# A two-layer hybrid decoder on one core: reciprocal roots of all norms taken by square root and reciprocal instead of by logarithm and exponential

## The chip, the core and the metric

The kernel runs on one core of a Trainium2 chip. The core has a matrix engine (TensorE, PE in the profile), a vector engine (VectorE, DVE), an engine for activation functions (ScalarE, ACT), a general engine (GpSimd, POOL) and queues that start DMA transfers (SyncE, SP). Each engine runs its own instructions in order and waits on semaphores for the others. The metric is the time of one execution on the device in microseconds; less is better.

## The reference, cut to what matters

The model has 512 tokens of width 1024 and two layers. Each layer normalizes its input, multiplies it by one wide matrix, runs four token mixers on groups of the result's columns, merges them under gates, multiplies by another matrix, normalizes and adds to the input; then comes a feed-forward part with two more norms.

```
h = rms_norm(x, norm_mix_pre[l]);  proj = h @ w_in[l]
y_a = hgrn2_mixer(...)      # ends in a norm over each head of 64
y_b = dsa_mixer(...)        # top-k attention, no norm
y_c = rwkv7_mixer(...)      # normalizes its keys, ends in a norm over each head
y_d = fox_mixer(...)        # attention with a forget gate, no norm
x = x + rms_norm(merged @ w_out[l], norm_mix_post[l])
hm = rms_norm(x, norm_mlp_pre[l]);  u = relu(hm @ w_up[l])
x = x + rms_norm(square(u) @ w_down[l], norm_mlp_post[l])

def rms_norm(t, g, eps=NORM_EPS):
    y = t * lax.rsqrt(jnp.mean(t * t, axis=-1, keepdims=True) + eps)
    return y * g
```

## The kernel before, in words

Everything is held transposed: features on the 128 partitions, tokens along the free dimension, so x is eight tiles of 128x512. Each matrix product in float32 is split into three products of rounded parts (high times high, low times high, high times low): lines 611, 612 and 613, on operands named `_hi` and `_lo`. Weights arrive in chunks of 128x1024; ScalarE writes their high part (line 1180), GpSimd their low part in four pieces (line 1641).

The large products ("dense" steps) are dealt out among the small ones of the mixers by a written table: `schedule()` and `FILL` say how many dense steps TensorE does between two small steps of a mixer. So TensorE mostly has dense work while VectorE and ScalarE prepare what a mixer's next small product needs, and stands idle only where the dense steps given to a place run out before that preparation is done.

A reciprocal root is needed at eight places in each layer:

- **Entry** (`norm_rstd(1, 1, 5, ...)` on ScalarE): 128x512 numbers for the norm of the layer's input. TensorE transposes the result (line 778), VectorE scales the first projections with it (lines 1804 and 1802, `taken_raw`), which also frees the PSUM banks that hold them.
- **Mixer A's norm** (lines 1394, 1395): 128x1024. VectorE writes the variances at line 1909 and multiplies with the result at line 1912, then finishes mixer A's output and turns to the rotations of mixer B (lines 1924 to 1926, TensorE's part at line 857).
- **Mixer C's keys** (lines 1444, 1445): 128x1024. VectorE goes on at line 2085 and builds the operands that TensorE transposes at line 915.
- **Mixer C's norm** (lines 1492, 1493): 128x1024, VectorE goes on at line 2157 and ends with `y_ready`, which TensorE needs before the products of branch 2.
- **After the mixers** (`norm_rstd(2, ...)` and `norm_rstd(3, ...)`): 128x256 each, one for each half of the tokens. VectorE's `residual_enter` scales (line 1744), adds to x (line 1749) and writes the low part of the next operand (line 1753), ScalarE its high part (line 1165).
- **After the feed-forward part** (`norm_rstd(4, ...)` and `norm_rstd(5, ...)`): the same, 128x256 each. In the first layer they lead into the next layer's entry, in the second into the output.

At each place ScalarE takes the logarithm (line 1271, for the first and the last two kinds), waits for its own result, and takes the exponential of minus one half of it (line 1272). ScalarE holds one set of function tables at a time; the compiler puts an `ACT_TABLE_LOAD` ahead of a function that the loaded set lacks. In the program as compiled such a load stands between the logarithm and the exponential at all eight places.

Of the kernel before, what the change touches and what calls it, by code (L numbers as in the profile page):

```python
# [12 lines left out]
LAYERS, T, D = 2, 512, 1024  # L13
# [254 lines left out]
def trunk_kernel(nc, x_in, wproj, wmerge, wrest, par_in, con_in, mask_in, rope_in, out):  # L268
    f32, f32r, u8 = mybir.dt.float32, mybir.dt.float32r, mybir.dt.uint8
    ALU, ACT = mybir.AluOpType, mybir.ActivationFunctionType  # L270
# [3 lines left out]
    with ctx:  # L274
        def sb(name, shape, dt=f32):
            return ctx.enter_context(nc.sbuf_tensor(name, shape, dt))
# [26 lines left out]
        slab = sb("slab", [P, 20, FT * T])  # L303
# [17 lines left out]
        rstd = sb("rstd", [P, T])  # L321
# [8 lines left out]
        ps = [ctx.enter_context(nc.psum_tensor(f"bank{i}", [P, 512], f32)) for i in range(8)]  # L330
# [70 lines left out]
        dve_took = signal("dve_took_dense", DVE0 + 16 * QUARTERS)  # L401
        relu_done = signal("relu_ready", 8 * QUARTERS)
        hid_hi = signal("hidden_hi_ready", 8 * QUARTERS)
        dve_step = signal("dve_step", 205)
        act_step = signal("act_step", 9)

        in_sq = signal("entry_squared", 2 * KT)
        entry_added = signal("entry_squares_added", 1)
# [8 lines left out]
        v_ready = signal("eps_term_ready", 1)  # L417
        o_total = signal("out_squares_added", 3)
        d_total = signal("down_squares_added", 2)
        rstd_done = signal("rstd_by_exp", 5)  # L420
        rstd_tr = signal("rstd_transposed", 1)
        rstd_col = signal("rstd_column_ready", 1)

# [26 lines left out]
        a_r = signal("a_rstd_ready", 1)  # L450
# [42 lines left out]
        c_kkr = signal("c_key_rnorm_ready", 1)  # L493
# [25 lines left out]
        c_rr = signal("c_rstd_ready", 1)  # L519
# [630 lines left out]
        def _(act):  # L1150
            fn = act.activation

            def link(ins, sig=act_step):

                ins.then_inc(*sig.up())
                act.wait_ge(*sig.at(L, sig.count))

            act.dma_start(par[:, 0:NPAR], par_in[0:1, :, 0:NPAR].rearrange("a p n -> (a p) n")).then_inc(par_first, 16)
            act.dma_start(con[:, 0:NHEAD], con_in[:, 0:NHEAD]).then_inc(ones_loaded, 16)
            act.preload_act_table(ACT.Ln)  # L1160
            act.wait_ge(par_first, 16)

            def split_x(m, n, hi, gain):
# [12 lines left out]
            with act.Fori(0, LAYERS) as L:  # L1176
# [49 lines left out]
                def take(place_):  # L1226
                    take_steps(TAKEN_TO[place_], REACH[place_] - TAKE_LAG)
# [40 lines left out]
                def norm_rstd(total, done, b, cols=slice(0, T), **bias):  # L1268

                    act.wait_ge(*sumsq.at(L, total))  # L1270
                    link(fn(rstd[:, cols], ps[b][:, cols], ACT.Ln, scale=1.0 / D, **bias))
                    fn(rstd[:, cols], rstd[:, cols], ACT.Exp, scale=-0.5).then_inc(*rstd_done.up())
                    assert rstd_done.count == done

                def attention(which, pt):
                    base = 16 * which
# [59 lines left out]
                act.dma_start(npre[:, :], par_in[bass.ds(act.snap(L * -1 + (LAYERS - 1)), 1), :, PC["pre"]:PC["pre"] + KT]  # L1336
                              .rearrange("a p n -> (a p) n")).then_inc(par_loaded.handle, 16)
                par_loaded.count += 32
                act.preload_act_table(ACT.Ln)
                split_to(INDEX[("aq", 0)] + 1)  # L1340
                norm_rstd(1, 1, 5, bias=C("eps", n=1))

# [46 lines left out]
                for t in range(FT):  # L1389
                    fn(S(19, t), S(18, t), ACT.Square).then_inc(*a_sq.up())  # L1390
                take(("a_norm", 0))
                act.preload_act_table(ACT.Ln)
                act.wait_ge(*a_var.at(L, 1))
                link(fn(slab[:, 0, :], slab[:, 0, :], ACT.Ln))
                fn(slab[:, 0, :], slab[:, 0, :], ACT.Exp, scale=-0.5).then_inc(*a_r.up())


                take("B")
# [3 lines left out]
                   scale=1.0 / 16.0).then_inc(*b_iwc.up())  # L1402
# [41 lines left out]
                link(fn(slab[:, 5, :], slab[:, 5, :], ACT.Ln))  # L1444
                fn(slab[:, 5, :], slab[:, 5, :], ACT.Exp, scale=-0.5).then_inc(*c_kkr.up())
# [44 lines left out]
                act.preload_act_table(ACT.Ln)  # L1490
                act.wait_ge(*c_vv.at(L, 1))
                link(fn(slab[:, 5, :], slab[:, 5, :], ACT.Ln))
                fn(slab[:, 5, :], slab[:, 5, :], ACT.Exp, scale=-0.5).then_inc(*c_rr.up())


                take("D")
# [40 lines left out]
                hi_part(o0 + 5)  # L1537
                out_taken(3)
                hi_part(o0 + 6)
                act.preload_act_table(ACT.Ln)  # L1540
                for m in range(4, KT):
                    out_taken(m, 0)
                    if m < 7:
# [54 lines left out]
                for j in range(13):  # L1598
# [5 lines left out]
                act.preload_act_table(ACT.Ln)  # L1604
                square(4, 0)
                hi_part(entry_order(CHUNKS + 0))
                square(5, 0)
# [81 lines left out]
        def _(dve):  # L1689
            tt, ts, stt = dve.tensor_tensor, dve.tensor_scalar, dve.scalar_tensor_tensor  # L1690

            def link(ins, sig=dve_step):

                ins.then_inc(*sig.up())
                dve.wait_ge(*sig.at(L, sig.count))
# [25 lines left out]
            with dve.Fori(0, LAYERS) as L:  # L1721
# [10 lines left out]
                def norm_lo(m):  # L1732

                    dve.wait_ge(*h_norm_hi.at(L, m + 1))
                    tt(hn[1][:, m, :], tmp[:, m % 4, :], hn[0][:, m, :].bitcast(f32), SUB).then_inc(*h_norm.up())

                def residual_enter(done, src, gain, part, split_gain, first, n, between={}):

                    cols = HALF[n]
                    dve.wait_ge(*rstd_done.at(L, done))  # L1740
                    base = [0] * KT

                    def scale(m):
                        stt(src[:, m, cols], src[:, m, cols], pcol(gain, m), rstd[:, cols], MUL, MUL).then_inc(*dve_step.up())  # L1744
                        base[m] = dve_step.count

                    def add(m):
                        dve.wait_ge(*dve_step.at(L, base[m]))
                        tt(x[:, m, cols], x[:, m, cols], src[:, m, cols], ADD).then_inc(*x_tiles.up())  # L1749

                    def lo(m):
                        dve.wait_ge(*h_hi.at(L, first + m + 1))
                        stt(part[1][:, m, cols], x[:, m, cols], gain_col(split_gain, m), part[0][:, m, cols].bitcast(f32), MUL, SUB)\  # L1753
                            .then_inc(*h_ready.up())
                    for m in range(KT + 2):
                        if m in between:
                            between[m]()
                        if m < KT:
                            scale(m)
                        if 0 < m <= KT:  # L1760
                            add(m - 1)
                        if m > 1:
                            lo(m - 2)
# [56 lines left out]
                tt(col[:, 6, 0:2], lb0, col[:, 5, 0:2], SUB)  # L1820
                tt(col[:, 6, 2:4], lb1, col[:, 5, 0:2], SUB).then_inc(*lb_in.up())
                ts(col[:, 5, 6:8], par[:, PC["ka"]:PC["ka"] + FT], -1.0, 1.0, MUL, ADD)
                dve.wait_ge(*rstd_done.at(L, 1))
                for i in range(2):
                    taken_raw("af", i)
                dve.wait_ge(*lb_exp.at(L, 1))
# [82 lines left out]
                    ins = ts(S(0, t), ps[4 + t][:, :], 1.0 / HD, EPS, MUL, ADD)  # L1909
                ins.then_inc(*a_var.up())  # L1910
                dve.wait_ge(*a_r.at(L, 1))
                link(tt(slab[:, 18, :], slab[:, 18, :], slab[:, 0, :], MUL))
                link(stt(slab[:, 18, :], slab[:, 18, :], pcol("hgw"), slab[:, 3, :], MUL, MUL))
                split(S(18), y[0][:, 0, :, :], y[1][:, 0, :, :], y_ready)
# [167 lines left out]
                dve.wait_ge(*c_exd.at(L, 1))  # L2082
                tt(slab[:, 6, :], slab[:, 6, :], slab[:, 12, :], MUL)
                dve.wait_ge(*c_kkr.at(L, 1))
                link(tt(slab[:, 4, :], slab[:, 4, :], slab[:, 5, :], MUL))
                link(tt(slab[:, 3, :], slab[:, 3, :], slab[:, 4, :], MUL))
                stt(slab[:, 7, :], slab[:, 7, :], -1.0, slab[:, 4, :], MUL, MUL)
# [261 lines left out]
```

## Time and profile before

| | |
|---|---|
| time, median of 3 runs | 2081.71 us (2080.02 to 2085.82) |
| the profiled execution's own time | 2085.43 us |
| its span, first to last instruction | 2083.5 us |
| TensorE's mean granted clock | 0.984 of full speed |
| TensorE busy | 1988.8 us (95% of the span) |
| VectorE, ScalarE, GpSimd busy | 997.4, 832.9, 999.1 us |

The busy shares are means over stages with different limits: an engine that is busy half of the time may still be the one that the others wait for in a given stretch. The idle time that the profile puts down to an instruction says which engine's result ended the wait. "L1272" is line 1272 of the kernel before.

### The profile page before, as it was taken

What the parts mean: (1) busy time and instruction counts of PE and PEld (TensorE: products, weight loads), DVE (VectorE), ACT (ScalarE), POOL (GpSimd) and SP (SyncE); (2) the same over time, 40 slices, a digit from 0 to 9 for tenths busy, and PEclk for the clock granted to TensorE, in tenths of its full rate; (3) what the DMA queues carried; (4) which work ended last, traced back from release to release, by engine and by line L of the source; (5) the groups of instructions that cost most, each with busy time, mean ns of one, the idle gap of its engine ahead of it and who ended that gap; (6) DMA issues with size and microseconds to landing.
All of it is one profiled execution on the core that took longest, in us unless ns stands there. A gap on an engine that the chain in (4) does not pass through costs nothing.

```text
span 2083.5 us, 34716 instructions
## 1 busy us (share of the span) xinstructions
PE 1988.8 (95%) x12444; PEld 1593.4 (76%) x12444; DVE 997.4 (48%) x1844; ACT 832.9 (40%) x1407; POOL 999.1 (48%) x1225
## 2 busy tenths in 40 slices
PE   7899999999999999999998999999999989999996
PEld 7786856777787888888887767577776788888885
DVE  6737976333433713223486479753234454223135
ACT  6434356324534422222463344642355263222235
POOL 4335525223566555557624444251253755555574
PEclk9999999999999999999999999999999999999998
DMA  5122311112132133233312223111121222333323
GB/s 177 60 82 69 94 52 41 42 32 62 62 108 73 60 105 101 91 101 93 111 48 72 82 71 92 42 46 37 32 71 62 91 82 72 111 96 96 101 91 122
DMA packets 53736, 163.09 MB, mean 78 GB/s; under 512 B 5312, under 2 KB 17728, under 8 KB 53312
## 3 DMA queue, kind: packets, MB, share of 16 engines
q1 hardware_dynamic: 52416, 158.09, 23.7%
q10 hardware_dynamic: 1152, 2.86, 0.4%
q8 instruction: 93, 1.52, 0.3%
q14 instruction: 75, 0.61, 0.1%
HBM read 158.83 MB, written 2.10 MB: 77 GB/s over the span
## 4 chain that ended last, share of the span: by engine, by line
issue 53%; POOL 44%; DVE 1%; POOLq 1%; ACT 1%; DMA 0%; PE 0%; SPq 0%; DVEq 0%; ACTq 0%
POOL w_lo L1641 38%; POOL slab L1665 3%; POOL slab L1686 1%; POOL wx_lo L1641 1%; POOL rstd L1654 1%; POOLq L1671 0%; POOL slab L1668 0%; DMA wx_raw<-wproj 0%; DVE slab L1744 0%; POOLq L1646 0%; DVE u_lo L1753 0%; ACT u_hi L1171 0%; ACT u_hi L1165 0%; POOL w_lo L1635 0%; DVE x L1749 0%
## 5 line engine op out<-in xcount | busy, mean ns | idle before, releaser
L1641 POOL TENSOR_TENSOR w_lo<-w_raw,w_hi 128x256 fp32r<-128x256 f32 x1104 | 853.5, 805 | 1046.9 <-ACT w_hi L1180 765.2
L611 PE MATMUL bank<-hn_hi,w_hi 128*128 128x512 f32 (+1 forms) x1312 | 538.7, 411 | 0.0
L613 PE MATMUL bank<-hn_hi,w_lo 128*128 128x512 f32 (+1 forms) x1312 | 508.5, 388 | 0.0
L612 PE MATMUL bank<-hn_lo,w_hi 128*128 128x512 f32 (+1 forms) x1312 | 508.5, 388 | 0.0
L611 PE MATMUL bank<-u_hi,w_hi 128*128 128x512 f32 (+1 forms) x864 | 306.5, 355 | 11.1 <-DVE u_lo L1767 5.7
L613 PE MATMUL bank<-u_hi,w_lo 128*128 128x512 f32 (+1 forms) x864 | 303.4, 351 | 0.0
L612 PE MATMUL bank<-u_lo,w_hi 128*128 128x512 f32 (+1 forms) x864 | 303.2, 351 | 0.0
L611 PEld LDWEIGHTS bank<-hn_hi,w_hi 128*128 128x128 f32 x1312 | 248.4, 189 | 71.0 <-issue 24.8
L613 PEld LDWEIGHTS bank<-hn_hi,w_lo 128*128 128x128 f32 x1312 | 248.4, 189 | 51.0
L1571 ACT ACTIVATE w_hi<-w_raw 128x1024 fp32r<-128x1024 f32 x120 | 127.3, 1061 | 399.3 <-DMA w_raw<-wrest 399.3
L612 PEld LDWEIGHTS bank<-hn_lo,w_hi 128*128 128x128 f32 x1312 | 249.1, 190 | 42.5 <-issue 3.4
L611 PEld LDWEIGHTS bank<-u_hi,w_hi 128*128 128x128 f32 x864 | 164.0, 190 | 37.7 <-DVE u_lo L1767 7.6
L612 PEld LDWEIGHTS bank<-u_lo,w_hi 128*128 128x128 f32 x864 | 164.1, 190 | 21.8 <-issue 0.5
L613 PEld LDWEIGHTS bank<-u_hi,w_lo 128*128 128x128 f32 x864 | 163.9, 190 | 21.4
L1180 ACT ACTIVATE w_hi<-w_raw 128x1024 fp32r<-128x1024 f32 x156 | 164.2, 1055 | 33.4 <-DMA w_raw<-wrest 17.1
L2230 DVE TENSOR_TENSOR slab<-slab,bank 128x512 f32<-128x512 f32 x56 | 38.5, 688 | 245.3 <-PE bank L613 245.3
L2221 DVE TENSOR_TENSOR tmp<-bank,tmp 128x512 f32<-128x512 f32 x64 | 44.2, 691 | 188.8 <-ACT tmp L1577 188.8
L1469 ACT ACTIVATE slab<-bank 64x128 f32<-64x128 f32 x160 | 43.7, 273 | 130.0 <-PE bank L962 128.1
L962 PEld LDWEIGHTS bank<-slab 64*64 64x64 f32 x1920 | 63.4, 134 | 32.1 <-issue 32.1
L1240 ACT ACTIVATE tmp<-bank 128x512 f32<-128x512 f32 x64 | 37.4, 600 | 119.1 <-PE bank L613 109.0
L2128 DVE COPY_PREDICATED slab<-msk,bank 128x256 f32<-128x256 uint8 x48 | 23.6, 491 | 115.6 <-PE bank L962 92.4
L962 PE MATMUL bank<-slab 64*64 64x32 f32 x1920 | 71.1, 220 | 2.1 <-DVE slab L2117 1.0
(346 smaller groups left out, 2853.5 us busy)
## 6 DMA issues: line engine op xcount, KB each, us to landing
w_raw<-wrest SPq DMA_DIRECT2D x140, 512.0 KB, 3.5
w_raw<-wmerge SPq DMA_DIRECT2D x80, 512.0 KB, 3.5
w_raw<-wproj SPq DMA_DIRECT2D x60, 512.0 KB, 3.5
wx_raw<-wproj SPq DMA_DIRECT2D x6, 512.0 KB, 5.3
slab<-rope ACTq DMA_DIRECT2D x2, 1024.0 KB, 5.4
wx_raw<-wrest SPq DMA_DIRECT2D x4, 512.0 KB, 5.0
out<-x SPq DMA_DIRECT2D x4, 512.0 KB, 3.0
x<-x_in SPq DMA_DIRECT2D x2, 512.0 KB, 9.8
```

Source lines behind the costliest of these rows:

```text
L611: mm(o_, stat[0], mov[0], start=first, stop=False)
L612: mm(o_, stat[0], mov[1], start=False, stop=False)
L613: return mm(o_, stat[1], mov[0], start=False, stop=last)
L962: ins = mm(packed(o_, n), stat[rs, cs_], halves(mov[rs, cs_], n, side), start=True, stop=True)
L1180: fn(wchunk(0, SLOT[c]), wload(SLOT[c]), ACT.Copy).then_inc(*w_hi_done.up(times))
L1240: ins = fn(tmp[:, i % 4, :], b_, ACT.Sigmoid)
L1469: ins = fn(into, from_, ACT.Copy)
L1571: fn(wchunk(0, s_), wload(s_), ACT.Copy).then_inc(*w_hi_done.up(times))
L1641: ins = pool.tensor_tensor(wchunk(1, s_)[:, cs], wload(s_)[:, cs], wchunk(0, s_)[:, cs].bitcast(f32), SUB)
L1665: pool.tensor_tensor(acc[:, m, :], acc[:, m, :], tmp[:, m % 4, :], ADD).then_inc(*merged.up())
L2221: tt(r_, ps[4 + m % 4][:, :], r_, MUL).then_inc(*dve_took.up(times))
L2230: tt(acc[:, m, :], acc[:, m, :], ps[4 + m % 4][:, :], ADD).then_inc(*dve_took.up(times))
```

## The change

On ScalarE the two functions become one square root; on VectorE a reciprocal of the same shape is put at the head of the work that uses the result, followed by a wait for its own result. The tables that ScalarE loads ahead of time are those of the square root instead of the logarithm. A new semaphore `root_done` tells VectorE that a root is there; `rstd_done`, which TensorE waits for at the entry, is now raised by VectorE.

```diff
 def norm_rstd(total, done, b, cols=slice(0, T), **bias):      # ScalarE
     act.wait_ge(*sumsq.at(L, total))
-    link(fn(rstd[:, cols], ps[b][:, cols], ACT.Ln, scale=1.0 / D, **bias))
-    fn(rstd[:, cols], rstd[:, cols], ACT.Exp, scale=-0.5).then_inc(*rstd_done.up())
+    fn(rstd[:, cols], ps[b][:, cols], ACT.Sqrt, scale=1.0 / D, **bias).then_inc(*root_done.up())
...
-act.preload_act_table(ACT.Ln)                                 # at six places ahead of a root
+act.preload_act_table(ACT.Sqrt)
...
 act.wait_ge(*a_var.at(L, 1))                                  # mixer A; the two of mixer C alike
-link(fn(slab[:, 0, :], slab[:, 0, :], ACT.Ln))
-fn(slab[:, 0, :], slab[:, 0, :], ACT.Exp, scale=-0.5).then_inc(*a_r.up())
+fn(slab[:, 0, :], slab[:, 0, :], ACT.Sqrt).then_inc(*a_r.up())
...
+def norm_rstd(done, cols=slice(0, T)):                        # VectorE
+    dve.wait_ge(*root_done.at(L, done))
+    link(dve.reciprocal(rstd[:, cols], rstd[:, cols]), rstd_done)
...
 def residual_enter(done, src, gain, part, split_gain, first, n, between={}):
-    dve.wait_ge(*rstd_done.at(L, done))
+    norm_rstd(done, cols)
...
-dve.wait_ge(*rstd_done.at(L, 1))                              # entry
+norm_rstd(1)
...
 dve.wait_ge(*a_r.at(L, 1))                                    # mixer A; the two of mixer C alike
+link(dve.reciprocal(slab[:, 0, :], slab[:, 0, :]))
 link(tt(slab[:, 18, :], slab[:, 18, :], slab[:, 0, :], MUL))
```

The order of ScalarE's instructions at mixer A's norm, before (ISA and REGISTER_ALU rows are waits and bookkeeping; `slab` holds the mixers' values):

```order
L1180 ACTIVATE w_hi<-w_raw 128x1024
L1392 ACT_TABLE_LOAD
L1393 REGISTER_ALU
L1394 ACTIVATE slab<-slab 128x1024
L1156 ISA
L1395 ACT_TABLE_LOAD
L1395 ACTIVATE slab<-slab 128x1024
```

and now, up to the next copy out of PSUM:

```order
L1181 ACTIVATE w_hi<-w_raw 128x1024
L1392 ACT_TABLE_LOAD
L1393 REGISTER_ALU
L1394 ACTIVATE slab<-slab 128x1024
L1237 ISA
L1184 ACTIVATE slab<-bank 128x512
```

The second function, its table load and the wait between the two are gone.

VectorE at the same place, before:

```order
L1907 ISA
L1909 TENSOR_SCALAR slab<-bank 128x512 x2
L1911 REGISTER_ALU
L1912 TENSOR_TENSOR slab<-slab 128x1024
L1695 ISA
```

and now:

```order
L1910 ISA
L1912 TENSOR_SCALAR slab<-bank 128x512 x2
L1914 REGISTER_ALU
L1915 RECIPROCAL slab<-slab 128x1024
L1692 ISA
L1916 TENSOR_TENSOR slab<-slab 128x1024
```

One reciprocal of 128x1024 and a wait for it stand ahead of the multiplication.

ScalarE at the last of the eight places (`norm_rstd(6, 5, ...)`, the second half after the feed-forward part), before:

```order
L1270 ISA
L1271 ACT_TABLE_LOAD
L1271 ACTIVATE rstd<-bank 128x256
L1156 ISA
L1272 ACT_TABLE_LOAD
L1272 ACTIVATE rstd<-rstd 128x256
L1594 ISA
L1165 ACTIVATE u_hi<-x,next_pre 128x256
```

and now:

```order
L1271 ISA
L1272 ACTIVATE rstd<-bank 128x256
L1591 ISA
L1166 ACTIVATE u_hi<-x,next_pre 128x256
L1167 ACTIVATE slab<-x 128x256
```

Two table loads go here, since only copies and squares stand between this root and the one before it. Over a layer ScalarE's table loads fall from 38 to 29, its eight exponentials go, and VectorE gets eight reciprocals: one of 128x512, three of 128x1024, four of 128x256.

## Rows read from the trace of the kernel before

**Rows 1.** The page, busy time of each engine with share of span and instructions.
```profile
PE 1988.8 (95%) x12444; PEld 1593.4 (76%) x12444; DVE 997.4 (48%) x1844; ACT 832.9 (40%) x1407; POOL 999.1 (48%) x1225
```
**Rows 2.** Waits of TensorE: total us, times, longest us.
```profile
PE bank L800 <- DVE slab L1882: 12.5, 2, 6.2
```
**Rows 3.** Groups by shape: busy us, mean ns; last row: min/median/max ns.
```profile
L1977 DVE RECIPROCAL col<-col 128x1 f32<-128x1 f32 x64 | 10.1, 157 | 5.0 <-ACT slab L1288 3.9
L1828 DVE RECIPROCAL col<-col 128x2 f32<-128x2 f32 x2 | 0.3, 166 | 0.1
L1821 DVE TENSOR_TENSOR col<-par,col 128x2 f32<-128x2 f32 x2 | 0.3, 148 | 0.0
...
L1272 ACT ACT_TABLE_LOAD  x10: 1283/1283/1283, 36.3 to 2067.7; - x10
```
**Rows 4.** Timeline at the entry: start, duration, engine, line [idle before, releaser].
```profile
35.61 0.69 ACT L1271 ACTIVATE rstd<-bank,con 128x512 f32<-128x512 f32 x1 [9.52 <-PE bank L682]
37.61 0.63 ACT L1272 ACTIVATE rstd<-rstd 128x512 f32<-128x512 f32 x1
38.37 1.29 DVE L1804 TENSOR_TENSOR slab<-bank,rstd 128x512 f32<-128x512 f32 x2 [6.06 <-ACT rstd L1272]
```
**Rows 5.** Timeline at mixer A's norm and the first rotations of mixer B.
```profile
150.04 1.06 ACT L1394 ACTIVATE slab<-slab 128x1024 f32<-128x1024 f32 x1 [3.62 <-DVE slab L1909]
152.42 1.06 ACT L1395 ACTIVATE slab<-slab 128x1024 f32<-128x1024 f32 x1
153.51 1.23 DVE L1912 TENSOR_TENSOR slab<-slab 128x1024 f32<-128x1024 f32 x1 [3.50 <-ACT slab L1395]
157.24 1.65 DVE L1767 TENSOR_TENSOR y_lo<-slab,y_hi 128x1024 fp32r<-128x1024 f32 x1
160.75 1.11 DVE L1926 TENSOR_TENSOR slab<-slab 128x512 f32<-128x512 f32 x1
161.92 1.13 PE L857 MATMUL bank<-slab,con 128*128 128x512 f32 x2
```
**Rows 6.** Timeline at mixer C's keys.
```profile
331.31 1.06 ACT L1444 ACTIVATE slab<-slab 128x1024 f32<-128x1024 f32 x1
334.77 1.36 DVE L2085 TENSOR_TENSOR slab<-slab 128x1024 f32<-128x1024 f32 x1 [3.78 <-ACT slab L1445]
336.69 7.95 POOL L1665 TENSOR_TENSOR slab<-slab,tmp 128x512 f32<-128x512 f32 x4
339.97 2.31 DVE L2088 TENSOR_TENSOR slab<-slab 128x1024 f32<-128x1024 f32 x1
345.78 5.38 PE L915 MATMUL bank<-con,slab 128*128 128x128 f32 x24 [3.25 <-DVE slab L2092]
```
**Rows 7.** Timeline at mixer C's norm and the first product of branch 2.
```profile
497.02 1.06 ACT L1492 ACTIVATE slab<-slab 128x1024 f32<-128x1024 f32 x1 [2.13 <-DVE slab L2154]
507.12 1.23 DVE L1767 TENSOR_TENSOR y_lo<-slab,y_hi 128x1024 fp32r<-128x1024 f32 x1
513.35 0.69 DVE L1783 TENSOR_TENSOR tmp<-bank,tmp 128x512 f32<-128x512 f32 x1 [3.44 <-PE bank L613]
```
**Rows 8.** Timeline after the mixers, after the feed-forward part and at the next entry.
```profile
685.23 0.39 PE L611 MATMUL bank<-hn_hi,wx_hi 128*128 128x256 f32 x1 [0.81 <-DVE hn_lo L1753]
...
1029.35 0.88 DVE L1744 SCALAR_TENSOR_TENSOR slab<-slab,par,rstd 128x256 f32<-128x256 f32 x2
...
1042.98 0.48 DVE L1753 SCALAR_TENSOR_TENSOR u_lo<-x,next_pre,u_hi 128x256 fp32r<-128x256 f32 x1 [1.66 <-ACT u_hi L1165]
...
1063.39 1.13 PE L682 MATMUL bank<-slab,con 128*128 128x512 f32 x2 [3.06 <-DVE slab L1810]
```
**Rows 9.** Stretches: length, busy us of PE, PEld, DVE, ACT, POOL, granted clock, DMA.
```profile
345.00:348.00 3.00, 2.22 (x11) 2.23 (x12) 0.89 (x2) 0.82 (x2) 3.00 (x4) 0.50 0.00 1
348.00:352.00 4.00, 3.31 (x17) 2.91 (x17) 0.18 (x1) 2.97 (x6) 0.37 (x1) 0.52 0.02 4
...
1064.00:1068.00 4.00, 3.96 (x30) 3.36 (x28) 2.01 (x5) 3.41 (x5) 2.69 (x4) 1.00 0.01 2
```

More of the change, by code:

```diff
@@ L403, in trunk_kernel @@
         hid_hi = signal("hidden_hi_ready", 8 * QUARTERS)
-        dve_step = signal("dve_step", 205)
-        act_step = signal("act_step", 9)
+        dve_step = signal("dve_step", 208)
+        act_step = signal("act_step", 1)
         in_sq = signal("entry_squared", 2 * KT)
@@ L419, in trunk_kernel @@
         d_total = signal("down_squares_added", 2)
-        rstd_done = signal("rstd_by_exp", 5)
+        root_done = signal("root_of_mean_square", 5)
+        rstd_done = signal("rstd_by_reciprocal", 5)
         rstd_tr = signal("rstd_transposed", 1)
@@ L1270, in norm_rstd @@
                     act.wait_ge(*sumsq.at(L, total))
-                    link(fn(rstd[:, cols], ps[b][:, cols], ACT.Ln, scale=1.0 / D, **bias))
-                    fn(rstd[:, cols], rstd[:, cols], ACT.Exp, scale=-0.5).then_inc(*rstd_done.up())
-                    assert rstd_done.count == done
+                    fn(rstd[:, cols], ps[b][:, cols], ACT.Sqrt, scale=1.0 / D, **bias).then_inc(*root_done.up())
+                    assert root_done.count == done
                 def attention(which, pt):
@@ L1338, in _ @@
                 par_loaded.count += 32
-                act.preload_act_table(ACT.Ln)
+                act.preload_act_table(ACT.Sqrt)
                 split_to(INDEX[("aq", 0)] + 1)
@@ L1391, in _ @@
                 take(("a_norm", 0))
-                act.preload_act_table(ACT.Ln)
+                act.preload_act_table(ACT.Sqrt)
                 act.wait_ge(*a_var.at(L, 1))
-                link(fn(slab[:, 0, :], slab[:, 0, :], ACT.Ln))
-                fn(slab[:, 0, :], slab[:, 0, :], ACT.Exp, scale=-0.5).then_inc(*a_r.up())
+                fn(slab[:, 0, :], slab[:, 0, :], ACT.Sqrt).then_inc(*a_r.up())
                 take("B")
@@ L1443, in _ @@
                 act.wait_ge(*c_kkv.at(L, 1))
-                link(fn(slab[:, 5, :], slab[:, 5, :], ACT.Ln))
-                fn(slab[:, 5, :], slab[:, 5, :], ACT.Exp, scale=-0.5).then_inc(*c_kkr.up())
+                fn(slab[:, 5, :], slab[:, 5, :], ACT.Sqrt).then_inc(*c_kkr.up())
                 fn(v1st[:, :, :].rearrange("p t n -> p (t n)"), slab[:, 14, :], ACT.Copy)
@@ L1489, in _ @@
                 take(("c_norm", 1))
-                act.preload_act_table(ACT.Ln)
+                act.preload_act_table(ACT.Sqrt)
                 act.wait_ge(*c_vv.at(L, 1))
-                link(fn(slab[:, 5, :], slab[:, 5, :], ACT.Ln))
-                fn(slab[:, 5, :], slab[:, 5, :], ACT.Exp, scale=-0.5).then_inc(*c_rr.up())
+                fn(slab[:, 5, :], slab[:, 5, :], ACT.Sqrt).then_inc(*c_rr.up())
                 take("D")
@@ L1539, in _ @@
                 hi_part(o0 + 6)
-                act.preload_act_table(ACT.Ln)
+                act.preload_act_table(ACT.Sqrt)
                 for m in range(4, KT):
@@ L1603, in _ @@
                         relu(0, last, j, 1)
-                act.preload_act_table(ACT.Ln)
+                act.preload_act_table(ACT.Sqrt)
                 square(4, 0)
@@ L1735, in norm_lo @@
                     tt(hn[1][:, m, :], tmp[:, m % 4, :], hn[0][:, m, :].bitcast(f32), SUB).then_inc(*h_norm.up())
+                def norm_rstd(done, cols=slice(0, T)):
+                    dve.wait_ge(*root_done.at(L, done))
+                    link(dve.reciprocal(rstd[:, cols], rstd[:, cols]), rstd_done)
+                    assert rstd_done.count == done
                 def residual_enter(done, src, gain, part, split_gain, first, n, between={}):
                     cols = HALF[n]
-                    dve.wait_ge(*rstd_done.at(L, done))
+                    norm_rstd(done, cols)
                     base = [0] * KT
@@ L2084, in _ @@
                 dve.wait_ge(*c_kkr.at(L, 1))
+                link(dve.reciprocal(slab[:, 5, :], slab[:, 5, :]))
                 link(tt(slab[:, 4, :], slab[:, 4, :], slab[:, 5, :], MUL))
@@ L2156, in _ @@
                 dve.wait_ge(*c_rr.at(L, 1))
+                link(dve.reciprocal(slab[:, 5, :], slab[:, 5, :]))
                 link(tt(slab[:, 3, :], slab[:, 3, :], slab[:, 5, :], MUL))
```

## The prediction, made before the changed kernel ran

> **What bounds the kernel now.** I read the page first, for who is busy: TensorE 95% of the span, the others under half of it [rows 1]. So time is lost only where TensorE idles or runs slowly, and work taken off ScalarE as such is worth nothing. The next view is TensorE's waits: the longest that recurs is 6.2 us in each layer, for VectorE's first scores of mixer A [rows 2]; VectorE runs up to it almost without a pause from the entry's norm on, so whatever moves the entry's norm moves that wait. Then I went through the timeline at each of the eight roots, and asked two things: when does VectorE get the reciprocal root, and how much dense work has TensorE left when the work behind it is done. The second layer has the same pattern some 1027 us later, so I work one layer out and double it.
>
> **What goes.** At each root ScalarE's path now is logarithm, table load (1283 ns, [rows 3]), exponential. At the 128x1024 roots the logarithm ends at 150.04 + 1.06 = 151.10, the exponential at 152.42 + 1.06 = 153.48 [rows 5]: 2.38 us go. At the entry it is 36.30 against 38.24 [rows 4], 1.94 us. A square root is taken to last as long as the logarithm of the same shape. Nine table loads and eight exponentials a layer go from ScalarE, some 17 us; nearly all of it lies under TensorE's dense work.
>
> **What is added: the price of a reciprocal.** The trace has none of these shapes. It has two small ones: one element 157 ns, two elements 166 ns, against 148 ns for the cheapest vector operation of two elements [rows 3]. That is 9 ns for the second element, and (166 - 148) / 2 = 9 ns for each above the floor, (157 - 148) = 9 for the one. An ordinary operation takes 1.23 us for 1024 elements [rows 7], 1.2 ns each. Bounds: from below an ordinary operation (0.42, 0.69, 1.23 us for 256, 512, 1024), from above 9.5 ns an element (2.6, 5.0, 9.9 us). The small rows are the same instruction and I go by them, a little under their slope since they jitter by several ns: 148 ns + 8.5 ns an element, so 2.3, 4.5 and 8.85 us.
>
> The Trainium skill speaks for it: VectorE: DVE Perf Modes, section "First, the fixed hardware budget", says that the reciprocal is an iterative divide with a repeat count of 8; with the 0.96 GHz of its Specifications that is an estimate of 8.3 ns an element, and the sum would come out some 2 us lower than mine.
>
> **Place by place, in one layer.**
> - *Entry.* The root ends at 36.30, the reciprocal at 36.30 + 0.07 + 4.5 = 40.9 instead of 38.24: VectorE starts 2.6 us late, and this passes down its chain into the wait of rows 2. Queued behind the reciprocal are the reads of the first projections (line 1804), which free PSUM banks, and TensorE's transposes; TensorE stops there too, but that only brings forward what it would wait later. **+2.6.**
> - *Mixer A's norm.* 151.15 + 8.85 = 160.0 against 153.48: VectorE 6.5 us late. The third rotation of TensorE at 161.92 needs VectorE's line 1926, which ends at 160.75 + 1.11 = 161.86 [rows 5]: no slack at all, and TensorE now doesn't idle there. Some comes back: VectorE's operations behind the norm are drawn out while GpSimd works (1.65 us for one that elsewhere takes 1.23, [rows 5, 7]; the first rotation likewise, 1.3 us in all), and GpSimd is done by 160. **+5.2** (up to 6.5).
> - *Mixer C's keys.* The root ends at 332.37, the reciprocal at 341.3 against 334.74: 6.5 us. TensorE waits there already (3.25 us, [rows 6]), so all of it counts. Here the relief is larger: six operations behind it last 10.9 us together, 7.5 at their undisturbed times (2.31 us against 1.23 for one of them), since four additions of GpSimd run beside them for 7.95 us [rows 6]. Two thirds of the 3.4 us come back. **+4.2** (3 to 6.5).
> - *Mixer C's norm.* 6.5 us again, 0.5 less for GpSimd. `y_ready` comes at 507.12 + 1.23 = 508.35; TensorE starts branch 2 at about 512.0, since VectorE gets its first unit at 513.35 [rows 7] and the unit takes 1.3. 3.65 us of slack cover part. **+2.6** (a bit over 6.0 - 3.65).
> - *After the mixers.* The first reciprocal (2.3 for 2.2 that go) changes nothing. At the second, ScalarE no longer spends two table loads and an exponential ahead of the high parts, and TensorE's wait of 0.81 us at 685.23 [rows 8] shrinks. The reciprocal itself starts when VectorE is through with the first half and is covered by TensorE's next 5.8 us of dense work. **-0.6.**
> - *After the feed-forward part.* The exponential ended before VectorE was ready at 1029.35 [rows 8], so nothing is won and the reciprocal is added: 2.3. Then the wait of 1.66 us for ScalarE at 1042.98 [rows 8] goes with its table loads, and the second reciprocal adds 2.3. VectorE's chain runs on into the sum that TensorE waits for at 1063.39, 3.06 us [rows 8], and in the second layer into the output. Less 0.4 for GpSimd. **+2.5.**
>
> Together 2.6 + 5.2 + 4.2 + 2.6 - 0.6 + 2.5 = 16.5.
>
> **The clock.** After the wait of 3.25 us at the keys TensorE's granted clock is 0.50 from 345 to 348 and 0.52 to 352 [rows 9], the lower of its two levels; some 6.5 us at half speed, 3.2 us lost where it has dense work. After the 3.06 us at 1063.39 it stayed at 1.00 [rows 9], so not each wait of three microseconds does it. The wait of five that is new at mixer A's rotations will, I take it: **+3.2**, and **+0.8** for one chance in four at mixer C's norm. At the entry a lower clock would be paid out of the wait of rows 2.
>
> Sum: 20.5 a layer, 41 in all. The profiled execution took 2085.4, so 2126.4 in its terms; it was 3.7 above the median of the three runs, so 2081.7 + 41 = **2123**.
>
> **Rivals.**
> 1. *The reciprocal costs what an ordinary operation does*, and the kernel is faster. Entry: 36.37 + 0.69 = 37.1 instead of 38.24, -1.2, all of it out of the wait of rows 2. Keys: 333.6 against 334.74, -1.1. Mixer A's norm and mixer C's norm: VectorE early, TensorE not waiting, 0. After the mixers -0.6. After the feed-forward part 0.45 - 1.66 + 0.45 = -0.8. That is -3.7 a layer, 2085.4 - 7.4 = 2078.0, or 2074 against the median. It decides from under 2.3 us for 128x1024: below that every place gains. Against it stand the 9 ns of the second element, for it that only 66 tiny instructions say so. The Trainium skill has this too: its Vector Engine (DVE) Microarchitecture Reference, section "3.2 Anatomy of a single slice", lets the divide chain span all eight slices, which as a pipeline would give an element a cycle. Chance 0.08.
> 2. *A middling price, 2.4 to 6 ns an element.* At 4 ns (1.2, 2.2, 4.2 us): entry +0.4, mixer A +1.1, keys +1.1, mixer C 0 since 3.65 us of slack hold, -0.6, and 0.7 after the feed-forward part: +2.7 a layer, 2087 against the median; at 2.4 it is no change, at 6 with a lower clock at mixer A some +18 in all, 2100. The same rows speak against it. Chance 0.15.
> 3. *The full price and nothing comes back*: 9.5 ns an element, GpSimd's work moves along with VectorE's, and the clock falls at mixer A's norm, mixer C's norm and behind the feed-forward part. 3.1 + 7.5 + 7.5 + 4 - 0.6 + 3.4 + 3 x 3.3 = 34.8, less what the last wait hides, 31: 2144. For it: four of the places follow on a wait that is there already. Chance 0.12.
>
> **How the numbers follow.** The forecast has 0.65; its own range is 2104 to 2140, from a slope of 7 ns without the clock's term to one of 9.5. The range given reaches from the middle of rival 2 to a little above rival 3: **2090 to 2146**, which leaves out rival 1, the lower half of rival 2 and the tails, some 0.18. 0.3% is 6.2 us, about what a measurement here can tell from none. Faster by more: most of rival 1, 0.06. Within: the rest of it and the cheap end of rival 2, 0.07. Slower: 0.87.
>
> **What the profile would show.** RECIPROCAL of 128x1024 at 8 to 9 us, of 128x512 near 4.5, of 128x256 near 2.3, each eight-fold of an ordinary operation; ScalarE's busy time down by some 34 us, VectorE's up by 80 less the relief. TensorE: a new wait of about 5 us at line 857 for VectorE, one of 2 to 3 at branch 2's first product, the one at line 915 grown from 3.25 to about 7, one at the entry's transposes, and the wait at line 682 above 3.06. VectorE's line 2088 well under 2.31 us. The mean granted clock slightly under 0.984. I am wrong if 128x1024 takes under 2.4 us, or if it takes 8 and TensorE doesn't wait at line 857.

## The result, and the profile after

The changed kernel takes 2105.86 us (median of 4 runs, 2104.74 to 2106.80) against 2083.77 (2080.02 to 2085.87) for the kernel before on the same chip: ratio 1.0105, 95% interval 1.0087 to 1.0124. It is slower by 22 us where 41 were forecast. The profiled execution took 2105.35 us, its span is 2103.5 against 2083.5, so the traces differ by 20.0. Every number below from a trace is of that execution, and layer 1 unless said.

The page of the changed kernel, busy time of each engine (before: [rows 1]):

```profile
PE 1991.4 (95%) x12444; PEld 1595.3 (76%) x12444; DVE 1059.3 (50%) x1860; ACT 801.1 (38%) x1373; POOL 991.6 (47%) x1225
```

ScalarE is relieved of 31.8 us, VectorE gets 61.9 more. TensorE's busy time grows by 2.6 us for the same instructions, so 17.4 of the 20.0 us are idle time of TensorE and 2.6 are a lower clock under its matmuls.

The new instructions, grouped by shape: busy us and mean ns behind the first bar, idle time before them and its releaser behind the second. Line 2162, mixer C's norm, has the mean of line 1915, and line 2089, the keys, one of 6552 ns. The small ones of [rows 3] are as before, 158 ns for one element:

```profile
L1737 DVE RECIPROCAL rstd<-rstd 128x256 f32<-128x256 f32 x8 | 14.0, 1748 | 1.6 <-ACT rstd L1272 1.6
L1915 DVE RECIPROCAL slab<-slab 128x1024 f32<-128x1024 f32 x2 | 13.1, 6554 | 2.3 <-ACT slab L1394 2.3
...
L1737 DVE RECIPROCAL rstd<-rstd 128x512 f32<-128x512 f32 x2 | 6.7, 3352 | 4.9 <-ACT rstd L1272 4.9
```

From 256 to 512 elements the price grows by 1604 ns, from 512 to 1024 by 3202: 6.27 and 6.25 ns an element, on a base of some 150 ns. At 1024 elements that is 5.3 times an ordinary operation's 1.23 us; the prediction spoke of eight-fold, though its own 8.85 us would be 7.2. By the Trainium skill (VectorE: DVE Perf Modes, "First, the fixed hardware budget") the estimate was 8.3 ns; the trace disagrees, and it disagrees too with the element per cycle that the divide chain over eight slices in the Trainium skill's Vector Engine (DVE) Microarchitecture Reference, "3.2 Anatomy of a single slice", would give as a pipeline.

TensorE's waits of the changed kernel: total us, times, longest us (rows 2 and the waits in rows 5, 6 and 8 answer to them):

```profile
PE bank L916 <- DVE slab L2097: 12.5, 2, 6.2
...
PE bank L801 <- DVE slab L1885: 9.9, 2, 4.9
PE bank L858 <- DVE slab L1930: 7.4, 2, 3.7
...
PE bank L683 <- DVE slab L1813: 4.4, 1, 4.4
...
PE bank L779 <- DVE rstd L1737: 1.4, 1, 1.4
```

The lines have moved by one or so: 801 was 800, 858 was 857, 916 was 915, 683 was 682. New is the wait at 858 (3.7 us per layer, at mixer A's third rotation); the keys' wait at 916 went from 3.2 to 6.2, the one at 683 from 3.1 to 4.4, and the one at the first scores (801) *fell* from 6.2 to 4.9. In layer 1, 1.4 us of it is now spent earlier, at the entry's transposes (779); in layer 2 there is no wait at 779, the wait at 683 ahead of them has grown by 1.4 instead, and TensorE runs at its lower clock level behind it (granted 0.50 from 1070.9 to 1077.7; the kernel before has 1.00 there, [rows 9]). No wait for `y_lo` of mixer C's norm is among them.

How late the changed kernel is, each row a start of the same matmul in both traces, in layer 1 unless the row says layer 2:

| point | before | after | late by |
|---|---|---|---|
| first scores of mixer A | 70.28 | 70.60 | 0.32 |
| mixer A's third rotation | 161.92 | 165.08 | 3.16 |
| product behind the keys | 345.78 | 352.56 | 6.78 |
| sum of squares after the mixers, last quarter | 678.30 | 685.48 | 7.18 |
| last wait for high and low parts of the first half, line 611 [rows 8] | 685.23 | 691.76 | 6.53 |
| entry of layer 2 | 1063.39 | 1072.05 | 8.66 |
| first scores of mixer A, layer 2 | 1099.22 | 1108.96 | 9.74 |
| product behind the keys, layer 2 | 1372.06 | 1391.95 | 19.89 |

So the two layers don't cost the same, 8.66 and 11.3 us. From the first scores to the keys' product layer 1 loses 6.46 and layer 2 10.15 us, with the same waits (3.69 and 6.2 us) in both: nearly all of the rest is how long TensorE runs at its lower clock level.

### The profile page after: what moved, and what is told of

Its sections match the earlier page's. It is cut to its first block, busy times and chain, and to the rows that moved or that the text cites. A ratio compares the mean times of both kernels' runs of the same rounds, so it can differ in the third digit from the quotient of the medians.

```text
span 2103.5 us, 34698 instructions
## 1 busy us (share of the span) xinstructions
PE 1991.4 (95%) x12444; PEld 1595.3 (76%) x12444; DVE 1059.3 (50%) x1860; ACT 801.1 (38%) x1373; POOL 991.6 (47%) x1225
## 4 chain that ended last, share of the span: by engine, by line
issue 54%; POOL 43%; DVE 1%; POOLq 1%; ACT 0%; DMA 0%; PE 0%; SPq 0%; DVEq 0%; ACTq 0%
POOL w_lo L1638 38%; POOL slab L1662 2%; POOL slab L1683 1%; POOL wx_lo L1638 1%; POOL rstd L1651 1%; POOLq L1668 0%; POOL slab L1665 0%; DMA wx_raw<-wproj 0%; DVE u_lo L1756 0%; POOLq L1643 0%; DVE slab L1747 0%; DVE rstd L1737 0%; ACT u_hi L1172 0%; POOL w_lo L1632 0%; DVE x L1752 0%
## 5 line engine op out<-in xcount | busy, mean ns | idle before, releaser
L612 PE MATMUL bank<-u_hi,w_hi 128*128 128x512 f32 (+1 forms) x864 | 305.4, 353 | 11.7 <-DVE u_lo L1770 5.9
```

The costliest lines, as they stand in the source:

```text
L612: mm(o_, stat[0], mov[0], start=first, stop=False)
```

## The experiments

**One place at a time.** Four kernels carry the change at one place only. Mixer A's norm:

```diff
+act.preload_act_table(ACT.Sqrt)          # for ACT.Ln
-link(fn(slab[:, 0, :], slab[:, 0, :], ACT.Ln))
-fn(slab[:, 0, :], slab[:, 0, :], ACT.Exp, scale=-0.5).then_inc(*a_r.up())
+fn(slab[:, 0, :], slab[:, 0, :], ACT.Sqrt).then_inc(*a_r.up())
...
 dve.wait_ge(*a_r.at(L, 1))
+link(dve.reciprocal(slab[:, 0, :], slab[:, 0, :]))
```

> Mixer A's norm alone takes root and reciprocal; the other seven places stay as before. By places: the reciprocal of 128x1024 lasts 6.55 us, VectorE is 6.55 + 0.05 - 2.4 = 4.2 us late, TensorE waits some 3.6 us at the third rotation in each layer, and some 3 us of lower clock follow at 1.5 us of loss each: +7 to +10 us. By the rival (the loss sits in where TensorE's clock falls, and single places don't add up): within 3 us of before although the wait at the rotations is there.

2090.83 us, ratio 1.0032 (1.0016 to 1.0048). TensorE's waits have the new one, up to 4.0 us; the others are as before, 6.2 us at line 800 and 3.2 at line 915:

```profile
PE bank L857 <- DVE slab L1926: 7.8, 2, 4.0
```

By the ratio mixer A's norm costs 6.7 us in both layers together, 3.3 (1.7 to 5) each, a little under the 7 to 10 that were expected. Its twelve runs lie between 2083.70 and 2098.27 and the profiled one is the slowest of them, so the wait is read from its trace and the price from the ratio. The spread goes with the granted clock of the run, 0.991 in the two fastest and 0.983 in the slowest; none of the 29 runs of the kernel before beside it has more than 0.988. At the same 0.988 this kernel takes 2087.20 and 2089.50 where the kernel before takes 2079.37 to 2080.47, which is 7 to 10 us, as expected. So the ratio holds a gain of clock in some runs; why they have it is open.

The keys alone, the same edit at `slab[:, 5, :]` ahead of `c_kkr`:

> Mixer C's keys alone. By places: the wait at the transposes of the keys' operands grows from 3.25 to some 6.2 us in each layer, +6 us in all, give or take 2 for the clock. By the rival: no more than 2 us, or as much as 10.

2093.17 us, ratio 1.0053 (1.0039 to 1.0068), 11 us: the dearest place, above the 6, give or take 2, that was expected. In its trace the wait grew by 3.0 us in the first layer and by 5.1 in the second, 8.1 of the 11. The two layers differ. VectorE and GpSimd behind the keys' reciprocal, first layer, then second (start, duration, [idle before, releaser]):

```profile
332.54 6.55 DVE L2084 RECIPROCAL slab<-slab 128x1024 f32<-128x1024 f32 x1 [1.40 <-ACT slab L1444]
335.86 6.03 POOL L1664 TENSOR_TENSOR slab<-slab,tmp 128x512 f32<-128x512 f32 x4
339.13 1.61 DVE L2085 TENSOR_TENSOR slab<-slab 128x1024 f32<-128x1024 f32 x1
...
341.85 5.72 POOL L1640 TENSOR_TENSOR w_lo<-w_raw,w_hi 128x256 fp32r<-128x256 f32 x4
...
348.91 4.35 PE L915 MATMUL bank<-con,slab 128*128 128x128 f32 x24 [6.24 <-DVE slab L2092]
...
1361.31 6.55 DVE L2084 RECIPROCAL slab<-slab 128x1024 f32<-128x1024 f32 x1 [1.41 <-ACT slab L1444]
1364.63 5.05 POOL L1664 TENSOR_TENSOR slab<-slab,tmp 128x512 f32<-128x512 f32 x4
1367.89 5.63 DVE L2085 TENSOR_TENSOR slab<-slab 128x1024 f32<-128x1024 f32 x1
1369.65 2.80 POOL L1640 TENSOR_TENSOR w_lo<-w_raw,w_hi 128x256 fp32r<-128x256 f32 x4
...
1379.78 3.46 PE L915 MATMUL bank<-con,slab 128*128 128x128 f32 x16 [8.35 <-DVE slab L2092]
```

GpSimd's additions start 3.32 us behind the reciprocal in both. In the first layer VectorE and GpSimd take turns, each drawn out (1.6 to 2.2 us for VectorE's 1.22, 11.7 us for GpSimd's eight). In the second one multiplication of VectorE lasts 5.63 us and ends 1.1 us after GpSimd's last operation (1369.65 + 2.80 = 1372.45), GpSimd does its eight in 7.85, and TensorE waits 8.35 instead of 6.24. The held multiplication is seen at the keys in one layer of this kernel, in one of the kernel with mixer A's reciprocal doubled and in both of the one with mixer C's doubled (below); in the changed kernel's own trace, in neither.

The Trainium skill has a rule for this (SBUF — State Buffer, "SBUF: two separate sides"): VectorE with two SBUF inputs and GpSimd lock a shared pair of ports for a whole instruction, and the other is blocked until it is free. The 5.63 us row fits the blocking; it spans several instructions of GpSimd, though, and in the first layer no operation of VectorE is held for more than 1 us. What decides between the two I did not settle.

Mixer C's norm alone, and the five roots of the model's own norms alone:

> Mixer C's norm alone. By places: VectorE is 4.2 us late, less 0.5 for GpSimd, and TensorE has 3.65 us of slack: no wait at branch 2, 0 us, give or take 2 for the clock. A rival in which every late reciprocal costs its lateness: +7 to +8 us.

2084.80 us, ratio 1.0009 (0.9998 to 1.0020), 2 us where 0, give or take 2, was expected, with no wait of TensorE at branch 2's first product.

> The five roots of the row norms (entry, two after the mixers, two after the feed-forward part) alone; the three of 128x1024 stay logarithm and exponential. By places, from the trace of the changed kernel: entry +0.1 to +1.1, after the mixers -0.65, after the feed-forward part +1.8 in each layer: +3.4 us. The four single changes should then add up to 7..10 + 6 + 0 + 3.4 = 17 to 20 us, against 20 in the spans of the two profiles. By the rival they don't add up.

2085.77 us, ratio 1.0012 (0.9999 to 1.0025), 2.5 us where 3.4 were expected. The first scores' wait is 9.9 us over two layers as in the changed kernel. Both are near nothing; with A and keys the four excesses are 0.0032 + 0.0053 + 0.0009 + 0.0012 = 0.0106, and the whole change has 0.0105. So the places add up, within what the intervals allow (about 0.003 on the sum), and that they would set off each other's waits or clock is not needed to explain the time. The near equality is in part luck: the keys' kernel has the held multiplication in one layer, the changed kernel in none.

**Twice the price at mixer A's norm.** A second reciprocal into a slab that is free, ahead of the one that counts:

```diff
 dve.wait_ge(*a_r.at(L, 1))
+link(dve.reciprocal(slab[:, 19, :], slab[:, 0, :]))
 link(dve.reciprocal(slab[:, 0, :], slab[:, 0, :]))
```

> The changed kernel with a second reciprocal of 128x1024 ahead of the one at mixer A's norm (its result goes to a tile nobody reads). By places: VectorE is already the last there, so all of 6.55 + 0.03 us passes to TensorE in each layer: the wait at the third rotation goes from 3.7 to 10.3 us, +13 us over the changed kernel, some +35 over before (ratio 1.017), give or take 3 for the clock.

2116.52 us, ratio 1.0160 (1.0133 to 1.0186); the changed kernel has 1.0105, so 6.55 us of VectorE per layer cost about 5.7 of the whole (5.0 by the two profiled spans, 2113.4 against 2103.5). The wait at the rotation:

```profile
PE bank L858 <- DVE slab L1931: 18.2, 2, 9.1
```

The wait at 858 grew by 9.1 - 3.7 = 5.4 us: once there is no slack, most of VectorE's 6.6 us there pass to TensorE. The expected 10.3 was a little high. The wait at 916 is up to 8.3 us, in the layer with the held multiplication.

**Twice the price at mixer C's norm**, where there is slack: the same edit with `slab[:, 7, :]` ahead of the reciprocal of `slab[:, 5, :]`.

> The same at mixer C's norm, where one reciprocal seemed to cost nothing. By places: the first used up the slack of 3.65 us almost to the end (VectorE was 4.2 - 0.5 late), so the second one shows in full: a wait of 6 to 6.6 us at branch 2 where there was none, +12 to +13 us over the changed kernel, ratio to before 1.016 to 1.017. If TensorE has more slack there than I read off, +8 or less.

2130.69 us, ratio 1.0236 (1.0210 to 1.0263): 27 us above the changed kernel by the two ratios, 24.0 by the two profiled spans, where 12 to 13 were expected. The slack is used up, as expected, but the wait behind it is 8.85, not 6 to 6.6. VectorE's chain from the second reciprocal to TensorE's product:

```profile
512.69 6.55 DVE L2163 RECIPROCAL slab<-slab 128x1024 f32<-128x1024 f32 x1
519.22 8.28 POOL L1638 TENSOR_TENSOR w_lo<-w_raw,w_hi 128x256 fp32r<-128x256 f32 x8 [8.24 <-ACT w_hi L1181]
519.28 1.75 DVE L2164 TENSOR_TENSOR slab<-slab 128x1024 f32<-128x1024 f32 x1
...
526.96 1.63 DVE L1770 TENSOR_TENSOR y_lo<-slab,y_hi 128x1024 fp32r<-128x1024 f32 x1
528.69 0.76 PE L612 MATMUL bank<-y_hi,w_hi 128*128 128x512 f32 x1 [8.85 <-DVE y_lo L1770]
```

In the changed kernel GpSimd is idle from 509.58 to 517.78, and `y_lo`, at 517.09, takes 1.23 us; here its low parts of the weights have moved beside the chain and draw out operations of 1.23 us to 1.62 to 1.75, some 2 us over the chain. Behind the wait TensorE's clock is at the lower level (the granted clock is the last number but two; in the kernel before it is 1.00 from 505 to 520, where its branch 2 starts, and from 524 to 532):

```profile
524.00:532.00 8.00, 3.31 (x8) 2.67 (x9) 6.07 (x9) 2.21 (x4) 3.50 (x4) 0.57 0.00 0
```

And the keys' wait, in both layers with the held multiplication, is 8.4 instead of 6.2. The two waits, 8.9 + 2.1 a layer, are 11 of the 12.0 us a layer between the profiled spans, and TensorE's busy time, which holds the clock, is 2.8 us longer over both layers (1994.2 against 1991.4). The expectation had the chain and the slack right, and missed what GpSimd's moved work does to the chain and to the keys.

**Are GpSimd's additions what draws VectorE out at the keys?** The changed kernel, with branch 1's additions on GpSimd cut to 8 of 512 columns (most of that branch's sum is left out):

```diff
-pool.tensor_tensor(acc[:, m, :], acc[:, m, :], tmp[:, m % 4, :], ADD)
+w_ = 8 if name == "branch1" else T
+pool.tensor_tensor(acc[:, m, 0:w_], acc[:, m, 0:w_], tmp[:, m % 4, 0:w_], ADD)
```

> The changed kernel with GpSimd's eight additions of branch 1 in a layer done on 8 columns instead of 512 (the rest of that sum is left out), four of which ran beside VectorE's chain behind mixer C's keys. By the theory that those additions draw VectorE's operations out: lines 2090 to 2093 fall from 1.6 to 2.2 us each to near 1.25, and TensorE's wait for line 2097 from 6.2 to 3.5 to 4.5 us: -4 to -5 us against the changed kernel, ratio to before some 1.008. By the rival (they are slow because of the reciprocal or of the weights' low parts): the four lines stay above 1.6 us and the time stays.

2108.90 us, ratio 1.0124 (1.0098 to 1.0150), where the changed kernel has 1.0105: no gain at all, and that expectation fell. VectorE at the keys:

```profile
340.89 0.67 POOL L1663 TENSOR_TENSOR slab<-slab,tmp 128x8 f32<-128x8 f32 x4
343.33 4.78 POOL L1638 TENSOR_TENSOR w_lo<-w_raw,w_hi 128x256 fp32r<-128x256 f32 x4 [1.76 <-ACT w_hi L1181]
344.16 1.68 DVE L2091 TENSOR_TENSOR slab<-slab 128x1024 f32<-128x1024 f32 x1
...
349.12 1.21 DVE L2094 TENSOR_TENSOR slab<-slab 128x1024 f32<-128x1024 f32 x1
```

The additions are as good as gone, but GpSimd's next work moves up beside the same operations, and they stay at 1.64 to 1.68 us until it ends at 348.11; the next takes 1.21. So it is no mark of the additions, nor of the reciprocal ahead: the weights' low parts do it as well. The wait at 916 fell by 1 us only, and TensorE's busy time is 2001.5 us against 1991.4, which is time at the lower clock.

**The other way to take load off ScalarE.** In the kernel before, a table load stands between each logarithm and its exponential [rows 3, 4]. The Trainium skill (ScalarE: Activation LUTs, "Table sets: the hidden batching unit") says that one set, `natural_log_exp_and_others`, holds both functions. This kernel keeps the logarithm and exponential and preloads that set by name:

```diff
-act.preload_act_table(ACT.Ln)        # 8 places; ACT.Exp ahead of mixer D's exponentials
+act.preload_act_table_set("natural_log_exp_and_others")
```

> The kernel before, with logarithm and exponential both from the one table set that holds both: it is loaded by name ahead of each logarithm, so no load stands between the two; ScalarE's loads fall from 38 to 25 a layer (by name also at mixer D's softplus), nothing is added on VectorE. By places: entry 1.28 us earlier out of the wait for the first scores; mixer A 0 (TensorE doesn't wait there); mixer C's keys 1.28 out of the wait of 3.25; mixer C's norm 0; after the mixers -0.6; after the feed-forward part the wait of 1.66 us on VectorE goes, -1.7. Together -3 to -4.9 a layer, -6 to -10 us in all, ratio 0.995 to 0.997. By the rival that only the clock's places matter: within 2 us.

2069.85 us, ratio **0.9941 (0.9923 to 0.9959)**: 12.3 us faster than the kernel before, more than the 6 to 10 that were expected, and by the two ratios 34 faster than the changed one. A layer has 25 table loads in place of 38. Mixer A's root, where the exponential now follows the logarithm at once (before: 2.38 us from end to end [rows 5], here 1.09), then the keys' product:

```profile
147.85 1.06 ACT L1394 ACTIVATE slab<-slab 128x1024 f32<-128x1024 f32 x1 [3.62 <-DVE slab L1909]
148.94 1.06 ACT L1395 ACTIVATE slab<-slab 128x1024 f32<-128x1024 f32 x1
...
336.99 1.91 PE L915 MATMUL bank<-con,slab 128*128 128x128 f32 x16
```

The wait of 3.25 us at that product [rows 6] is gone, where 1.28 was expected to go: two table loads go ahead of it, the one between the functions and the one that stood ahead of the logarithm (in the kernel before from 330.01 to 331.29). The wait at the first scores is 5.5 for 6.2. The clock falls behind this product too, but for less: it is at the lower level from 341.9 to 345.3, and in the kernel before from 345.0 to 351.8 [rows 9].

A stretch of 20 us before the keys differs likewise. From 270 to 290 TensorE's granted clock is 1.00 here and 0.83 before. The kernel before first, then the one with mixer C's norm changed alone, which has the same instructions as before up to that norm, some 490 us on:

```profile
270.00:290.00 20.00, 17.89 (x82) 10.42 (x82) 15.78 (x47) 8.87 (x24) 3.99 (x6) 0.83 0.08 27
```

```profile
270.00:290.00 20.00, 17.88 (x97) 10.75 (x96) 18.32 (x54) 10.30 (x28) 5.41 (x6) 1.00 0.08 26
```

With the same instructions the low clock is there in one trace and not in the other. The kernel with the keys changed alone, on the same chip as the second row and with the same instructions up to 330 us, has it again, from 277.0 to 283.8. So in this stretch it goes with the execution and not with the code, and that this kernel's clock is higher is not shown to be its doing.

By the profiled spans it is 16.3 us shorter: 8.4 us less busy time of TensorE for the same matmuls, which is clock, and 7.9 less idle time, which is the waits and within the 6 to 10 of the expectation. The profiled execution of the kernel before lies 3.7 us above its median, at a granted clock of 0.984, so part of the 8.4 may be chance.

## Why the prediction was right in kind and twice too large

The direction, the mechanism and the place that first shows it held: a long reciprocal on VectorE where TensorE has no slack, a new wait at mixer A's third rotation, a doubled one at the keys. The time was 17 us below the forecast, 22 us of loss for 41: the price of the reciprocal was set too high, the clock's term too, and part of the price was absorbed at the entry and at mixer C's norm.

- **The price of a reciprocal** is the term that was mis-sized: 148 ns + 8.5 ns an element was taken, 150 + 6.25 measured, so 6.55 us for 8.85 at 1024 elements, 3.35 for 4.5, 1.75 for 2.3. The slope came from the step between two tiny rows, 157 and 166 ns, over a floor of 148. The floor was another instruction's; with 6.25 ns the same rows give 151 and 154, a spread well within what such short rows hide. The 2.3 us less at each 1024-wide root is what takes the other terms down. With the measured price in its own steps the sum is 1.5 + 2.9 + 1.9 + 0 - 0.6 + 1.4 = 7.1 us a layer, and 10.3 with the 3.2 of the clock: 14 to 21 us in all for the measured 22. That this comes so near is partly luck, since its entry and its clock are too high and its mixer A and keys too low, as follows.
- *Entry, +2.6.* With the measured price VectorE starts its reads at 40.02 for 38.37 [rows 4], 1.65 late. But the first scores are only 0.32 late. The sigmoid's table load and the first function behind it, before:

```profile
39.30 1.28 ACT L1198 ACT_TABLE_LOAD   x1
40.60 0.63 ACT L1198 ACTIVATE slab<-slab 128x512 f32<-128x512 f32 x1
```

  and the changed trace:

```profile
35.81 0.69 ACT L1272 ACTIVATE rstd<-bank,con 128x512 f32<-128x512 f32 x1 [9.51 <-PE bank L683]
36.53 3.35 DVE L1737 RECIPROCAL rstd<-rstd 128x512 f32<-128x512 f32 x1 [3.95 <-ACT rstd L1272]
38.98 1.28 ACT L1199 ACT_TABLE_LOAD   x1
40.02 1.29 DVE L1807 TENSOR_TENSOR slab<-bank,rstd 128x512 f32<-128x512 f32 x2
```

  The load of the sigmoid's table, which VectorE's chain meets next, now runs, all but 0.4 us, under the reciprocal, and the function behind it starts at 40.74 for 40.60. The step treated the chain from the entry to the scores as VectorE's alone; it passes through ScalarE, and there the lateness was absorbed.
- *Mixer A's norm, +5.2.* From the end of ScalarE's first function to VectorE's multiplication it is 157.26 - 150.64 = 6.6 us for 153.51 - 151.10 = 2.4, so 4.2 late, less relief. The rows:

```profile
149.58 1.06 ACT L1394 ACTIVATE slab<-slab 128x1024 f32<-128x1024 f32 x1 [3.62 <-DVE slab L1912]
150.67 6.55 DVE L1915 RECIPROCAL slab<-slab 128x1024 f32<-128x1024 f32 x1 [1.13 <-ACT slab L1394]
154.40 2.83 POOL L1638 TENSOR_TENSOR w_lo<-w_raw,w_hi 128x256 fp32r<-128x256 f32 x4 [6.87 <-ACT w_hi L1181]
157.26 1.22 DVE L1916 TENSOR_TENSOR slab<-slab 128x1024 f32<-128x1024 f32 x1
158.08 5.48 POOL L1638 TENSOR_TENSOR w_lo<-w_raw,w_hi 128x256 fp32r<-128x256 f32 x4 [0.86 <-ACT w_hi L1181]
161.35 1.63 DVE L1770 TENSOR_TENSOR y_lo<-slab,y_hi 128x1024 fp32r<-128x1024 f32 x1
165.08 1.13 PE L858 MATMUL bank<-slab,con 128*128 128x512 f32 x2 [3.69 <-DVE slab L1930]
```

  3.69 us of wait, and 3.6 us of lateness from the root on; the relief was 0.6 and not 1.3, since GpSimd works here until 163.56 (the two POOL rows), not until 160, and `y_lo` still takes 1.63. The trace of before could have warned of it: GpSimd is at work there until 164.29.

```profile
154.99 9.30 POOL L1641 TENSOR_TENSOR w_lo<-w_raw,w_hi 128x256 fp32r<-128x256 f32 x8 [6.99 <-ACT w_hi L1180]
```

  The chain was right (no slack, new wait), its relief was not.
- *Keys, +4.2.* The wait went from 3.25 to 6.23, +3.0. With 6.55 us the reciprocal comes 4.2 later than the exponential; two thirds of the drawing-out were to come back (2.3), 1.2 did. The forecast took it that GpSimd's four additions would mostly be over when VectorE came; they were not: GpSimd works through from 339.52 on, additions first and weights behind (6.02 + 5.72 us), and the four operations that follow the reciprocal take 1.61, 2.19, 1.63 and 1.74.

```profile
336.20 6.55 DVE L2089 RECIPROCAL slab<-slab 128x1024 f32<-128x1024 f32 x1 [1.40 <-ACT slab L1443]
339.52 6.02 POOL L1662 TENSOR_TENSOR slab<-slab,tmp 128x512 f32<-128x512 f32 x4
342.79 1.61 DVE L2090 TENSOR_TENSOR slab<-slab 128x1024 f32<-128x1024 f32 x1
...
345.51 5.72 POOL L1638 TENSOR_TENSOR w_lo<-w_raw,w_hi 128x256 fp32r<-128x256 f32 x4
```

- *Mixer C's norm, +2.6.* Nothing: `y_lo` ends 13.6 us behind the root's end, for 10.3 before [rows 7], so it is 3.4 late (4.2 less 0.8 for GpSimd) against a slack of 3.65. No wait of TensorE's matmuls comes of it; the weight load of branch 2 at 518.39 had stood idle for 0.37 us.

```profile
504.70 6.55 DVE L2162 RECIPROCAL slab<-slab 128x1024 f32<-128x1024 f32 x1 [1.12 <-ACT slab L1490]
517.09 1.23 DVE L1770 TENSOR_TENSOR y_lo<-slab,y_hi 128x1024 fp32r<-128x1024 f32 x1
```

  The slack was read rightly, as the doubled norm shows: 6.55 us more and TensorE waits.
- *After the mixers, -0.6.* Right: 7.18 late ahead of it, 6.53 behind, and the wait of 0.81 is 0.15.
- *After the feed-forward part, +2.5.* 8.66 - 6.53 = +2.1. The wait at line 682 grew, as forecast, from 3.06 to 4.42. For ScalarE's squares TensorE waits 2.64 us at once (line 689, at 1043.87) where the trace of before has two waits, 1.34 and 1.20.
- **The clock, +4 a layer.** It does fall behind mixer A's new wait, but not at once and for less: 3.4 us, first row below. TensorE's busy time, which holds this, grew by 2.6 us in the whole run, not 8.

```profile
166.40:169.80 3.40, 3.40 (x10) 2.62 (x9) 2.95 (x5) 1.25 (x2) 0.00 (x0) 0.50 0.06 8
350.70:357.50 6.80, 4.94 (x23) 4.94 (x24) 1.97 (x4) 2.77 (x5) 0.52 (x1) 0.50 0.01 2
```

  The second row is the stretch at the keys: though that wait is twice as long as it was, the clock is low for 6.8 us as before (345.0 to 351.8 there), and it falls 1.9 us before the wait's end. The term rests on one execution. In the kernel with mixer C's norm changed alone the same wait of 3.25 us, with the same code up to there, is followed by a low clock of 3.4 us only:

```profile
343.00:347.00 4.00, 3.57 (x19) 3.17 (x17) 0.00 (x0) 3.12 (x6) 1.75 (x3) 0.57 0.01 4
```

Of the rivals, the ordinary price (a kernel that gets faster) and the full price of which nothing comes back are out. The middling price is nearest: it ran to 6 ns and gave 2100 there. 6.25 ns and 2105.9 lie just past its end, on the cheap side of the forecast's own range. Rows that jitter by several nanoseconds could not tell 6 from 9 ns an element; that was the reason to give this rival more than 0.15.

## What to carry to other kernels

A reciprocal of a whole tile on VectorE (6.25 ns an element here) takes longer than the table load and exponential that it replaces as soon as the tile is wider than some 250 elements (an estimate from these rows): at 256 both are about 1.7 us, at 1024 2.4 went and 6.55 came. Whether that costs time is decided by TensorE's slack at the place: 3.65 us of it took all of mixer C's lateness. Before moving work off ScalarE, look whether its two functions share a table set and load that set by name; here that alone won 0.6%. Don't price an operation by the difference of two rows that last 150 ns, and don't count on relief when GpSimd's work moves along: a delay that is made on VectorE brings other work of GpSimd beside the chain.

## What the runs showed of the hardware

- VectorE's reciprocal in f32: 1748, 3352 and 6554 ns for 256, 512 and 1024 elements a partition. Over all traces those of 1024 lie between 6552 and 6555 ns, those of 256 between 1743 and 1754, also while GpSimd worked beside them (the rows at 336.20 and 339.52).
- A square root and a logarithm on ScalarE last the same: 1.06 us for 128x1024, 0.69 for 128x512 out of PSUM. A table load is 1283 ns in every trace.
- VectorE's two-input operations of 128x1024 beside GpSimd's two-input ones take 1.6 to 2.3 us for 1.22, or one is held for 5.63 us while GpSimd runs at its full pace. With the same distance between reciprocal and additions both are seen, and the second costs TensorE 2.1 us more.
- The time varies by 10 us between executions of the same program (2079.37 to 2089.40 over 29 runs of the kernel before), and it goes with the mean granted clock of TensorE: 0.988 in the seven fastest, 0.983 in the three slowest. Of the clock, each trace shows one execution; what sets the stretches at the lower level was not found. Whether the keys' two patterns change between executions of one program was not measured.
